# Flow-matching trunk step in float32: gate/up products of the feed-forward block as seven half-size block products, with weight sums and g_lo on GpSimd

## What is computed

```python
def swiglu(h, w_in, w_out):
    g, u = jnp.split(h @ w_in, 2, axis=-1)
    return (jax.nn.silu(g) * u) @ w_out

hp = modulate(rms_norm(xp, norm2_w[i]), mod_p[3], mod_p[4])
hs = modulate(rms_norm(xs, norm2_w[i]), mod_s[3], mod_s[4])
xp = xp + mod_p[5] * swiglu(hp, ffn_in_w[i], ffn_out_w[i])
xs = xs + mod_s[5] * swiglu(hs, ffn_in_w[i], ffn_out_w[i])
```

## Time and profile before

| | |
|---|---|
| time, median of 3 runs | 2666.12 us (2665.93 to 2666.26) |
| profiled execution, its own time | 2665.85 us |
| its span | 2664.2 us |
| TensorE busy | 2651.6 us, 17638 matmuls |
| VectorE busy | 1718.7 us |
| ScalarE busy | 862.8 us |
| GpSimd busy | 94.0 us |
| granted TensorE clock, mean | 0.998 |
| DMA | 294.95 MB, mean 111 GB/s |

### The profile page before, as it was taken

How to read it: one execution, slowest core, us unless ns; L and a number is a source line. 1 busy time by engine, 2 the same in 40 slices (tenths; PEclk the granted TensorE clock), 3 DMA queues, 4 the chain that set the end, 5 groups by cost and what they waited for, 6 DMA issues and landing times.

```text
span 2664.2 us, 45828 instructions
## 1 busy us (share of the span) xinstructions
PE 2651.6 (100%) x17638; PEld 2581.8 (97%) x17638; DVE 1718.7 (65%) x2908; ACT 862.8 (32%) x1185; POOL 94.0 (4%) x185
## 2 busy tenths in 40 slices
PE   9999999999999999999999999999999999999998
PEld 5999999999999999999968999999999999999998
DVE  5898778686587777746675778676465554334345
ACT  4223332322342122125665431322332233233122
POOL 0000001000000000000000001000000000000000
PEclk9999999999999999999999999999999999999999
DMA  8443345344223444422002235443122212222212
GB/s 308 142 146 138 127 140 174 124 162 132 77 85 129 161 144 134 142 67 86 33 13 88 96 133 174 132 144 119 64 87 71 79 64 79 79 71 71 79 65 70
DMA packets 85604, 294.95 MB, mean 111 GB/s; under 512 B 10112, under 2 KB 13312, under 8 KB 85248
## 3 DMA queue, kind: packets, MB, share of 16 engines
q1 hardware_dynamic: 60016, 200.74, 22.5%
q0 software_dynamic: 25488, 92.81, 10.4%
HBM read 290.63 MB, written 2.88 MB: 110 GB/s over the span
## 4 chain that ended last, share of the span: by engine, by line
PE 96%; DVE 2%; ACT 1%; DMA 1%; issue 0%; DVEq 0%; ACTq 0%; SPq 0%
PE ps L464 45%; PE ps L465 45%; PE ps_x L678 1%; PE ps L654 1%; PE ps L810 1%; PE ps_sum L665 1%; DMA mix<-in_ada_head 1%; DVE w_lo L1236 1%; PE ps L761 0%; ACT w_hi L872 0%; PE ps L535 0%; PE ps_sum L640 0%; DVE g_lo L1250 0%; ACT g_hi L884 0%; DVE tmp L1312 0%
## 5 line engine op out<-in xcount | busy, mean ns | idle before, releaser
L1236 DVE TENSOR_TENSOR w_lo<-raw,w_hi 128x1024 fp32r<-128x1024 f32 (+2 forms) x359 | 429.1, 1195 | 634.0 <-ACT w_hi L872 632.0
L872 ACT ACTIVATE w_hi<-raw 128x1024 fp32r<-128x1024 f32 (+2 forms) x359 | 371.9, 1036 | 973.2 <-PE ps L465 967.1
L464 PE MATMUL ps<-h_hi,w_hi 128*128 128x320 f32 x1888 | 590.2, 313 | 0.7 <-DVE h_lo L1396 0.7
L465 PE MATMUL ps<-h_lo,w_hi 128*128 128x322 f32 x1888 | 586.5, 311 | 0.0
L464 PE MATMUL ps<-h_hi,w_lo 128*128 128x320 f32 x1888 | 586.3, 311 | 0.0
L465 PE MATMUL ps<-h_hi,w_lo 128*128 128x322 f32 x1888 | 585.8, 310 | 0.0
L465 PE MATMUL ps<-h_hi,w_hi 128*128 128x322 f32 x1888 | 584.6, 310 | 0.0
L464 PE MATMUL ps<-h_lo,w_hi 128*128 128x320 f32 x1888 | 583.9, 309 | 0.0
L1264 DVE CUSTOM_DVE_ANT_0 ps_x<-ada_w,cond 128x1024 f32<-128x1024 f32 x354 | 435.9, 1231 | 28.5 <-DVE tmp L1312 13.2
L465 PEld LDWEIGHTS ps<-h_hi,w_hi 128*128 128x128 f32 x1888 | 359.0, 190 | 0.6
L465 PEld LDWEIGHTS ps<-h_hi,w_lo 128*128 128x128 f32 x1888 | 358.2, 190 | 0.0
(11 more groups left out here) (179 smaller groups left out, 2887.9 us busy)
## 6 DMA issues: line engine op xcount, KB each, us to landing
raw<-in_weights SPq DMA_DIRECT2D x323, 512.0 KB, 3.3
ada_w<-in_ada_w POOLq DMA_DIRECT2D x177, 512.0 KB, 3.5
raw<-in_weights SPq DMA_DIRECT2D x32, 384.0 KB, 3.0
mix<-in_ada_head SPq DMA_DIRECT2D x16, 512.0 KB, 10.3
x<-in_x SPq DMA_DIRECT2D x8, 320.0 KB, 9.9
out_y<-mix SPq DMA_DIRECT2D x16, 160.0 KB, 1.9
mix<-in_spread SPq DMA_DIRECT2D x1, 1088.0 KB, 5.5
cond<-in_cond SPq DMA_DIRECT2D x1, 1024.0 KB, 13.6
```

Source lines behind the costliest of these rows:

```text
L464: pe.matmul(ps[:, 2 * slot, 0:TA], w[:, slot, ws], a(k)[:, 0:TA], start=begin, stop=end)
L465: mm = pe.matmul(ps[:, 2 * slot + 1, 0:width - TA], w[:, slot, ws], a(k)[:, TA:width], start=begin, stop=end)
L872: act.activation(w_hi[:, j % 2, 0:tiles * P], raw[:, j, 0:tiles * P] if src is None else src, ACT.Copy).then_inc(w_hi_ready, 1)
L1236: dve.tensor_tensor(w_lo[:, j % 2, 0:tiles * P], raw[:, j, 0:tiles * P] if src is None else src, w_hi[:, j % 2, 0:tiles * P].bitcast(F32), ...
```

## The change

Eleven of the twelve gate/up chunks, 80 of 88 pairs (all but chunk 0 of the pooling layer), compute gate and up rows by a scheme of seven block products in place of eight. The gate and up weights of a pair are cut in input halves (A11, A12 gate; A21, A22 up; four feature tiles each), the h rows in input halves and token halves (B11, B12; B21, B22, of 322 columns, of which the first half uses 320). With

- S1 = A21 + A22, S2 = S1 - A11, S3 = A11 - A21, S4 = A12 - S2 of the weights, 128x512 each,
- T1 = B12 - B11, T2 = B22 - T1, T3 = B22 - B12, T4 = T2 - B21 of the rows, 128x322 for each of four tiles,

the seven products are P1 = A11 B11, P2 = A12 B21, P3 = S4 B22, P4 = A22 T4, P5 = S1 T1, P6 = S2 T2, P7 = S3 T3 (4 tiles x 3 passes = 12 matmuls each, into one bank), and the results P1 + P2, P1 + P6 + P5 + P3, P1 + P6 + P7 - P4, P1 + P6 + P7 + P5 are gate and up of the two token halves. P6, P7 and P4 are added into P1's bank, P3 into P5's; the sign of P4 is in how T4 is made.

- **TensorE** runs the products of pair p in the order P1, P4 of pair p-1, P5, P6, P2, P7, P3.
- **GpSimd** makes the four S of a pair, the T rows (but the last tile's), and `g_lo` (`hidden_lo`). The loads of `ada_w` are written out between: in a chunk with sums the triple of pairs 2, 4 and 6 stands behind the S4 of that pair.
- **ScalarE** and **VectorE** split seven blocks of 512 columns a pair in place of two tiles of 1024. `w_hi`/`w_lo` now hold four places of 512; a block is refilled when the product that used its place is done (`REFILL`). ScalarE also keeps P1, P5 and P1 + P6 from the banks, VectorE adds the others to them and scales.
- `mix` shares its place with the T rows (`turned`, and `mix` itself for their full values); loops over quads are written out.

```diff
-ROW = T + 4
+ROW = T + 8
+TW = TA + 2
+HALF = KD // 2
+HW = HALF * P
+def _order(n):
+    out = [(0, 1), (0, 5), (0, 2), (0, 6), (0, 3), (0, 7)]
+    for p in range(1, n):
+        out += [(p, 1), (p - 1, 4), (p, 5), (p, 6), (p, 2), (p, 7), (p, 3)]
+    return out + [(n - 1, 4)]
+FIRST_SEVEN = [1 if kind == "pool" else 0 for kind in KIND]
...
@@ gpsimd
+            def t234_of(layer, k):
+                n, m = 2 * layer + 1, HALF + k
+                pool.wait_ge(h_ready, H_BASE[n] + m + 1)
+                pool.wait_ge(t_lo_ready, T_STEPS * layer + k + 1)
+                own(pool.tensor_tensor(t3_full[:, k, :], h_hi[:, m, TA:TH].bitcast(F32), h_lo[:, m, TA:TH].bitcast(F32), ALU.add), steps)
+                own(pool.tensor_tensor(t2_full[:, k, :], t3_full[:, k, :], t2_full[:, k, :], ALU.subtract), steps)
...
+            def s13(layer, c, p, q, n, norm):
...
+                pool.tensor_tensor(s1_home(p, norm), up_w[:, 0:HW], up_w[:, HW:2 * HW], ALU.add).then_inc(s_made, 1)
+                pool.wait_ge(block_lo_ready, SEVEN * first + PLACE[n][p, 1] + 1)
+                pool.wait_ge(s_made, 4 * (first + p) + 1)
+                pool.tensor_tensor(up_w[:, 0:HW], gate_w[:, 0:HW], up_w[:, 0:HW], ALU.subtract).then_inc(s_made, 1)
+            def s24(layer, c, p, n, norm):
+                first, j = _pairs_before(layer, c), 2 * (p % 2)
+                gate_w = raw[:, j, :]
+                pool.wait_ge(s_made, 4 * (first + p) + 2)
+                pool.tensor_tensor(gate_w[:, 0:HW], s1_home(p, norm), gate_w[:, 0:HW], ALU.subtract).then_inc(s_made, 1)
+                pool.wait_ge(block_lo_ready, SEVEN * first + PLACE[n][p, 2] + 1)
+                pool.wait_ge(s_made, 4 * (first + p) + 3)
+                pool.tensor_tensor(gate_w[:, HW:2 * HW], gate_w[:, HW:2 * HW], gate_w[:, 0:HW], ALU.subtract).then_inc(s_made, 1)
+            def hidden_lo(g, p):
+                pool.wait_ge(g_hi_ready, g + p + 1)
+                pool.tensor_tensor(g_lo[:, p, :], up_row(p)[:, 0:T], g_hi[:, p, :].bitcast(F32), ALU.subtract).then_inc(g_ready, 1)
+            def rest_of_chunk(layer, c, q, n, norm, triples):
+                g = LAYER_G[layer] + G_MIX[KIND[layer]] + CHUNK * c
+                for p in range(1, n):
+                    s13(layer, c, p, q, n, norm)
+                    s24(layer, c, p, n, norm)
+                    if p % 2 == 0 and p // 2 < len(triples):
+                        ada_triple(triples[p // 2])
+                    hidden_lo(g, p - 1)
+                hidden_lo(g, n - 1)
...
@@ tensor, seven_chunk
+                def product(p, m, out, a_hi, a_lo, begin, row_ready=None):
+                    b = place[p, m]
+                    pe.wait_ge(block_lo_ready, SEVEN * first + b + 1)
+                    hi, lo = block_home(w_hi, n, b), block_home(w_lo, n, b)
+                    for k in range(HALF):
+                        if row_ready is not None:
+                            pe.wait_ge(h_ready, row_ready + k + 1)
+                        ws = slice(k * P, k * P + P)
+                        for i, (w, a) in enumerate(((hi, a_hi), (hi, a_lo), (lo, a_hi))):
+                            mm = pe.matmul(out, w[:, ws], a[:, k, :], start=begin and k == 0 and i == 0,
+                                           stop=k == HALF - 1 and i == 2, skip_group_check=True)
+                    mm.then_inc(seven_done, 1)
...
@@ vector
+            def block_lo(n, b, norm, first):
+                p, m = ORDER[n][b]
+                dve.wait_ge(block_hi_ready, SEVEN * first + b + 1)
+                dve.tensor_tensor(block_home(w_lo, n, b), block_source(p, m, norm), block_home(w_hi, n, b).bitcast(F32),
+                                  ALU.subtract).then_inc(block_lo_ready, 1)
...
+                def modulation(p, e):
+                    if p // 2 < len(ada):
+                        ada_share(ada[p // 2], 3 * (p % 2) + e, 3 * (p % 2) + e + 1)
+                def after_p1(p):
+                    refill(p, 1)
+                    modulation(p, 0)
...
+                for p in range(1, n):
+                    after_p1(p)
+                    after_p4(p - 1)
+                    refill(p - 1, 4)
+                    hidden(p - 1)
+                    refill(p, 5)
+                    after_p6(p)
+                    after_p2(p)
+                    after_p7(p)
...
+                    after_p3(p)
```

More of the change, by code:

```diff
@@ new lines, in _, with t1_of @@
+            steps = [0]
+            def t1_of(layer, k):
+                n = 2 * layer + 1
+                pool.wait_ge(h_ready, H_BASE[n] + k + 1)
+                pool.tensor_tensor(t2_full[:, k, :], h_hi[:, k, TA:TH].bitcast(F32), h_lo[:, k, TA:TH].bitcast(F32), ALU.add)
+                own(pool.tensor_tensor(t4_full[:, k, :], h_hi[:, k, 0:TW].bitcast(F32), h_lo[:, k, 0:TW].bitcast(F32), ALU.add), steps)
+                pool.tensor_tensor(t2_full[:, k, :], t2_full[:, k, :], t4_full[:, k, :], ALU.subtract).then_inc(t1_made, 1)
@@ L852, in _ @@
                     tiles = CHUNK if c < 2 else LAST
-                    h_quads(q, 2 * layer + 1, tiles // 2, first=(c == 0), late=(c == 0 and kind == "pool"))
+                    if c < FIRST_SEVEN[layer]:
+                        h_quads(q, 2 * layer + 1, tiles // 2, first=True, late=True)
+                    else:
+                        seven_chunk(layer, c, q, tiles, c == 0)
                     q += tiles // 2
@@ L910, in out_quad @@
+            def out_quad(q, m0, n, tiles, squares, folds=True, first=None, turns=None):
                 for j in range(4):
@@ L914, in out_quad @@
                         step(q, j, tiles[j])
+                        if first is not None and j >= 2:
+                            first_blocks(*first, j)
                     if squares:
@@ L921, in out_quad @@
                         step(q, j, tiles[j])
+                        if first is not None:
+                            first_blocks(*first, j)
+                    if turns is not None:
+                        turn_step(turns, j)
             def fold_hi(m, n):
@@ L1350, in out_quad @@
+            def out_quad(q, m0, n, gate, tiles, squares, folds=True, ada=None, triples=1, first=None, turns=None):
                 for j in range(4):
```

504 lines of the change are left out of this document (441 added, 63 removed).

## The result

| | us | range | runs |
|---|---|---|---|
| before | 2666.02 | 2665.83 to 2666.26 | 4 |
| changed | 2931.41 | 2930.51 to 2932.49 | 4 |
| forecast | 2875 | 2620 to 2935 | |

What follows compares the result with a forecast made beforehand. TensorE bound the kernel; seven products would save 141.6 us, but VectorE and GpSimd taking turns at the SBUF would cost more: 2665.9 - 141.6 + 264 + 56 + 31 = 2875 us, range 2620 to 2935 (8 in 10).

Steps and rivals of the forecast that it cites:

- turns at the SBUF: VectorE's two-SBUF-operand instructions and GpSimd's SBUF reads exclude each other: 5.0 us a pair with adaLN sums, less 0.44.
- the rival without turns: Engines read SBUF side by side, GpSimd hides under TensorE, only the load wait binds: 2632 us, faster; chance 0.21.
- A chunk with sums: Chunk whose pairs also make adaLN sums on VectorE: 19.0 us a pair against TensorE's 12.39, +38.7 us a chunk.
- 82% of GpSimd's time falls on it: In pairs with sums, 0.82 of GpSimd's 6.07 us, 5.0 us, delays VectorE, by VectorE's share of two-SBUF-operand work.
- The load wait: VectorE stands 4.7 us for adaLN loads issued behind the fourth weight sum, three times a chunk: 1.75 us a pair.
- GpSimd's price: A two-input GpSimd operation takes 1.16 us for 512 columns (0.95 to 1.38 bounds) and 1.43 for 640.
- The pair without sums: Forty pairs without adaLN sums take 13.8 us each, against TensorE's 12.39.
- 7.22 and 6.07 make 13.3 at the least: In pairs without sums, VectorE's two-operand work and GpSimd's time exclude each other and add to at least 13.3 us.
- Starts: 18 + 5 + 8: Seven-product starts: +18 late h rows (layers 0, 2, 3), +5 low parts in unit steps, +8 T sums on GpSimd.
- 54 sums, 0.77 us each, mostly under slack: GpSimd's T sums before the starts, with turns at the SBUF, cost some 8 us more.
- What would have shown it: Listed signs: subtractions well above 686 ns, TensorE idle a quarter of chunks with sums, load waits 3.5 us or more.
- chunks of 150 us: Sign of being right: chunks in layers 0 and 2 take 150 us (113 before), in layer 3 about 110.

Runs made afterwards that it cites:

- experiments 1 and 2: Changed kernel, GpSimd's weight sums and g_lo made memsets of one column (1) or full width (2), T sums full-width memsets in both: 2700.4 and 2703.1 us.
- experiment 1: Changed kernel with GpSimd's weight sums and g_lo made one-column memsets and its T sums full-width memsets: 2700.4 us (1.0130).
- experiment 3: Changed kernel with the three adaLN loads of pairs 2, 4 and 6 issued before the fourth weight sum: 2870.2 us (1.0769).
- experiment 8: Changed kernel with GpSimd's sums of T rows made memsets of the same 322 columns, weight sums and g_lo kept: 2876.5 us (1.0790).
- experiment 10: Seven products only in the last layer's last two chunks, T rows made ahead, weight sums and g_lo on VectorE, otherwise kernel before: 2650.8 us (0.9943).
- experiment 9: Seven products only in the last layer, weight sums and g_lo on VectorE, T sums on GpSimd, otherwise kernel before: 2663.1 us (0.9989).

## Why the prediction was right, and where it was wrong

**Sign and mechanism were right.** The forecast rested on turns at the SBUF; experiments 1 and 2 show them (231 us go with GpSimd's sums, next to nothing with its writes), and the rival without turns is out. The Trainium skill, SBUF — State Buffer, section "Who interferes with whom", says that a VectorE instruction with two SBUF inputs contends with a GpSimd instruction that reads SBUF and not with one that only writes it. The trace agrees: 1.23 us became 2.86 beside two sums of 0.90 and 0.89, and 688 ns stayed 688 beside memsets.

**That the time lies in the range is partly luck.** 2931 is 4 us below its upper end. The terms of a chunk with sums cancel, and the pairs without sums hide 16 of the 66 us by which the starts were priced too low.

**A chunk with sums: +38.6 against +38.7 us, by errors that cancel.** That is 19.0 us a pair, as forecast; the 19.3 between two triples has a load in every second pair, a chunk in three of eight. VectorE alone needs 12.9 us, not 12.7: with all on VectorE a pair takes 16.42, of which the four sums and g_lo are 3.48 by their distance from start to start. GpSimd's sums cost (38.6 - 10.1) / 8 = 3.6, against experiment 1, where the forecast had 5.0 - 0.44 = 4.6. There the step "82% of GpSimd's time falls on it" failed: a share of busy time says nothing of whether both are at it at the same time. VectorE was lengthened by 2222.4 - 1948.9 (busy in experiment 1) = 273.5 us, 3.4 a pair. The load wait was nearly right: VectorE stands 5.3 us in place of 4.7, and experiment 3 gives back 12.4 us a chunk, 1.6 a pair, where the forecast had 1.75. The 0.9 that is left (already seen in experiment 1, where a pair with sums but no load takes 13.5 us) was not forecast, and no run takes it apart.

**GpSimd's price.** 1.28 us alone for 512 columns (2485 to 2495 us, layer 3) and 1.54 for 640, forecast 1.16 and 1.43; within the bounds of 0.95 and 1.38. The Trainium skill, GPSIMD Engine Reference, section 3.1, gives 4497 ns for 2048 columns; a quarter of it is 1.12 us, an estimate (the prediction's 1.15 is a little above), and the measurement is 14% over that.

**The pair without sums: 13.18, forecast 13.8.** "7.22 and 6.07 make 13.3 at the least" added listed durations. The next instruction starts 0.60 us after one listed at 0.68 (372.64 and 373.24 in the changed kernel), so the parts that exclude each other are shorter than the lists. Over the 40 pairs with their chunk ends the changed kernel is 30.2 us faster than before, forecast 14: 16 us to the good. TensorE's own 12.39 us came out as 12.50 where nobody is late (experiment 1).

**The term that failed: "Starts: 18 + 5 + 8".** Against a later chunk of the same kind the start chunks lose 66.0 - 38.4, 64.1 - 38.4, 59.3 - 38.8 and 12.3 + 11.0: 97 us for 31. That is the whole error: 66 too little here, 16 too much in the pairs without sums, 6 in small parts (2.1 in the pooling layer's first chunk, 2.3 ahead of layer 3's). Three things were left out. (a) The T sums: "54 sums, 0.77 us each, mostly under slack", 8 us, cost 55 (experiment 8). The changed kernel makes 108 of them, 27 at each of four starts, at 0.88 us alone and 1.18 in the mean. In the start VectorE has no slack, and each row goes from GpSimd to ScalarE to VectorE in series. (b) The pooling layer's start, priced at nothing but the common turns, costs 25.7. (c) TensorE's clock. The three overlap (16 of the 55 us lie in the pooling layer, and without the T sums' reads the granted clock of the whole run rose from 0.95 to 0.96), so they don't add up to the 66. The waits of TensorE at layer 3's start, and what came behind the first:

```profile
2473.47 0.60 PE L749 MATMUL ps<-h_hi,w_hi 128*128 128x322 f32 x1 [6.29 <-issue]
2473.87 0.47 PE L749 MATMUL ps<-h_lo,w_hi 128*128 128x322 f32 x1
2474.14 0.47 PE L749 MATMUL ps<-h_hi,w_lo 128*128 128x322 f32 x1
2474.41 0.47 PE L749 MATMUL ps<-h_hi,w_hi 128*128 128x322 f32 x1
...
2482.30 0.56 PE L749 MATMUL ps<-turned,w_hi 128*128 128x322 f32 x2 [4.46 <-ACT tmp L1294]
```

After 6.3 us of idleness the matmuls start 270 ns apart and not 147: the lower level, 1.2 GHz. In four start windows of the changed kernel (193 us, granted 0.70, 0.70, 0.76, 0.82) TensorE is idle for 70.7 us and busy for 122.3 with 587 recorded matmuls, which at 147.5 ns would take 86.6: by this estimate some 36 us go to the clock. (Some records may be missing, so it is an upper figure.) The forecast had idle time only, and only the first 5 to 7 us of it.

**What would have shown it** was mostly there: subtractions at 933 ns, load waits of 5.3 us in the mean, T rows waited for longer than 7 us (10.0 in layer 1). TensorE idles for 29 of 127 us in the chunk with sums, just under a quarter. Of the "chunks of 150 us" only the later ones came out so, 113.0 + 38.4 = 151; the first ones take 113 + 66 = 179 in layer 0, and layer 3's second takes 102 and not 110.

## What to carry to other kernels

Before work is moved to GpSimd to relieve VectorE, look at which of VectorE's instructions read two SBUF tensors at the moment when the moved one will run: where VectorE stands idle the move gains at most its own duration (7 us here, of the 33 that forty g_lo take); where it doesn't, the two wait for each other, and 770 us of GpSimd sums cost 231. Ask what stands behind the moved instruction in the new engine's queue, and what it will wait for there; three DMA issues behind a sum cost 61 us, and g_lo ahead of the next pair's sum went with 12. And price a gap of TensorE with what the matmuls behind it cost at the lower clock, and make start-up work a stage ahead: in experiment 10 it was free there.

## What the runs showed of the hardware

GpSimd's writes to the SBUF (527 ns for 512 columns, 635 for 640) don't hold VectorE up at all: 688 and 1229 ns beside them, 2.7 us between experiments 1 and 2. The turns are by whole instructions, not by halves: in the example above each of the two engines once stood for the other's full time, and VectorE for two GpSimd sums in a row. VectorE instructions that read a product bank and one tensor in the SBUF are not lengthened: of the 320-column updates of `x`, 27 lie mostly beside GpSimd's sums in the changed kernel, and none takes over 0.55 us (0.545 in experiment 1). A two-input GpSimd operation takes about 1.9 times VectorE's (1.28 against 0.69 us for 512 columns). What stays open: in experiment 9 the eleven unchanged chunks and stages before layer 3's own are each some 0.3 us longer than in the kernel before (pairs at 14.24 for 14.20), 3.8 us in all; no run tells whether that is the row pitch or the longer program.
